# One expert matrix kept in eight pieces in idle rows of the mixer, and its ring slot given to another matrix

## The reference

```
u = rms_norm(x, norm_mix_g[l]) @ w_in[l]
o_a = differential_attention(aq, ak, av, ...)
o_b = hgrn2(bq, bf, bi, bg, lower_bounds[l], hgrn_norm_g[l])
o_c = short_conv(cb, cc, cx, conv_w[l])
x = x + concatenate([o_a, o_b, o_c]) @ w_out[l]
h = rms_norm(x, norm_ffn_g[l])
# each token: one of 4 groups, in it 2 of 8 experts
y_e = (silu(h @ w_gate[e]) * (h @ w_up[e])) @ w_down[e]
x = x + sum of gates * y_e over the token's two experts
```

## Time and profile before

| what | value |
|---|---|
| median of three runs | 1191.2 us |
| the profiled execution's own time | 1192.3 us |
| its span, first to last instruction | 1190.2 us |
| PE busy | 885.7 us, 74% of the span |
| DVE busy | 505.8 us, 42% |
| ACT busy | 171.2 us, 14% |
| POOL busy | 36.9 us, 3% |
| bytes moved | 442.22 MB, mean 372 GB/s |

### The profile page before, as it was taken

How to read it: one execution, slowest core, us unless ns; L and a number is a source line. 1 busy time by engine, 2 the same in 40 slices (tenths; PEclk the granted TensorE clock), 3 DMA queues, 4 the chain that set the end, 5 groups by cost and what they waited for, 6 DMA issues and landing times.

```text
span 1190.2 us, 20391 instructions
## 1 busy us (share of the span) xinstructions
PE 885.7 (74%) x8533; PEld 531.0 (45%) x8533; DVE 505.8 (42%) x1307; ACT 171.2 (14%) x479; POOL 36.9 (3%) x75
## 2 busy tenths in 40 slices
PE   9999997774657574756799999976757575746557
PEld 6577475342324242424465675643424232423234
DVE  2977464332414242424339674643324142424233
ACT  2334211100000000000013441101000000000000
POOL 2011000000000000000000120000000000000000
PEclk9999998888978788978799999988888797888888
DMA  8946389999999999999996273899999999999996
GB/s 276 388 188 249 133 330 426 429 425 428 428 428 428 428 429 428 427 430 425 414 389 260 72 282 124 349 430 427 427 427 428 427 430 428 428 429 428 428 425 282
DMA packets 54700, 442.22 MB, mean 372 GB/s; under 512 B 9312, under 2 KB 12400, under 8 KB 29296
## 3 DMA queue, kind: packets, MB, share of 16 engines
q1 hardware_dynamic: 54640, 441.36, 89.5%
HBM read 440.30 MB, written 1.05 MB: 371 GB/s over the span
## 4 chain that ended last, share of the span: by engine, by line
PE 60%; DMA 27%; DVE 9%; issue 2%; ACT 1%; SPq 1%; DVEq 0%
DMA ring<-in_expert_w_up 26%; PE psum L820 15%; PE psum L835 8%; PE psum L854 8%; PE psum L863 6%; PE psum L938 5%; PE psum L720 5%; PE psum L794 4%; DVE work L1470 2%; PE psum L811 1%; DVE work L1481 1%; PE psum L886 1%; PE psum L955 1%; DVE work L1476 1%; PE psum L738 1%
## 5 line engine op out<-in xcount | busy, mean ns | idle before, releaser
L820 PE MATMUL psum<-ring,work 128*32 128x256 f32 x3712 | 247.8, 426 | 102.9 <-DMA ring<-in_expert_w_up 101.3
L835 PE MATMUL psum<-ring,work 128*32 128x256 f32 x1664 | 144.6, 505 | 131.2 <-DVE work L1476 125.7
L820 PEld LDWEIGHTS psum<-ring,work 128*32 128x32 f32 x3712 | 138.9, 124 | 212.0 <-issue 156.7
L835 PEld LDWEIGHTS psum<-ring,work 128*32 128x32 f32 x1664 | 62.1, 137 | 202.2 <-DVE work L1476 147.8
L1468 DVE TENSOR_SCALAR work<-work 128x128 f32<-128x128 f32 x62 | 14.1, 227 | 312.8 <-ACT work L1142 312.8
L1481 DVE COPY work<-psum 32x256 f32<-32x256 f32 x124 | 52.6, 424 | 158.4 <-PE psum L835 157.3
L854 PE MATMUL psum<-ring,hT 128*128 128x512 f32 x224 | 98.5, 594 | 1.7 <-ACT work L1165 1.7
L720 PE MATMUL psum<-work,h 128*128 128x128 f32 x512 | 66.0, 291 | 32.5 <-DVE work L1434 26.5
L1146 ACT ACTIVATE work<-psum 32x256 f32<-32x256 f32 x124 | 46.2, 373 | 289.1 <-PE psum L835 288.4
L720 PEld LDWEIGHTS psum<-work,h 128*128 128x128 f32 x512 | 62.9, 204 | 45.8 <-DVE work L1434 36.9
L863 PE MATMUL psum<-hT,ring 128*128 128x256 f32 x320 | 70.7, 380 | 0.0
(11 more groups left out here) (289 smaller groups left out, 774.9 us busy)
## 6 DMA issues: line engine op xcount, KB each, us to landing
ring<-in_expert_w_gate SPq DMA_DIRECT2D x64, 2048.0 KB, 18.3
ring<-in_expert_w_up SPq DMA_DIRECT2D x62, 2048.0 KB, 22.6
ring<-in_expert_w_down SPq DMA_DIRECT2D x52, 2048.0 KB, 23.1
ring<-in_w_in SPq DMA_DIRECT2D x10, 2048.0 KB, 18.1
work<-in_expert_w_down SPq DMA_DIRECT2D x6, 2048.0 KB, 21.1
ring<-in_w_out SPq DMA_DIRECT2D x4, 2048.0 KB, 8.1
ring<-in_w_in SPq DMA_DIRECT2D x8, 512.0 KB, 13.4
maps<-in_expert_w_down SPq DMA_DIRECT2D x2, 2048.0 KB, 8.5
```

What stands on the lines that cost most here:

```text
L820: last = T.matmul(bank[GU_BANK[i % 2]][CAP * j:CAP * j + CAP, 0:2 * P], xg[:, k, CAP * i:CAP * i + CAP], gate_up[:, :, k, P * j:P * j + P] ...
L835: last = T.matmul(bank[5][CAP * q:CAP * q + CAP, 0:2 * P], actT[i % 2][:, CAP * j:CAP * j + CAP], down[j][:, 2 * P * q:2 * P * q + 2 * P], ...
```

## The change

In the mixer of each layer SP starts five more transfers. They bring the up matrix of expert 0 in tiles of 512 columns (one for each k of 8) to `up_rows`: rows 4, 5, 7, 11 and 12 of `u` (part of `work`), the two halves of `masks`, and a new tensor `spare`. The first four wait for `lev_sb`, count 9 (the last copy under the masks), the fifth for `oat_ps`, count 2 (`oa_transposes(1)`).

The slot that held up0 now gets gate3, loaded in the mixer at the place in the list where up0 was loaded. Before, gate3 was loaded into slot 2 after the gate product of expert 1. So slot 2 is free earlier, and experts 4 to 7 are placed and ordered anew: gate4 takes that slot, down4 waits for down step 0 alone, down6 waits for up step 4.

```
-        FIRST = [SET_A, (2, AHEAD, IN_MAPS), (0, 1, IN_WORK), (2, XTRA, IN_MAPS)]
-        SECOND = [SET_A, SET_C, SET_B, SET_A]
+        FIRST = [(3, IN_ROWS, 5), (2, AHEAD, IN_MAPS), (0, 1, IN_WORK), (4, XTRA, IN_MAPS)]
+        SECOND = [(2, 3, 5), SET_C, SET_B, SET_A]
+        SECOND_ODD = [(3, 2, 5)] + SECOND[1:]
...
                 e.wait_ge(proj_ps.sem, proj_ps.after(l, projected("bf")))
-                part(ring_full, place(l, FIRST[0][1]), 0, 1)
+                part(ring_full, place(l, FIRST[3][0]), 3, 0)
...
                 part(ring_full, place(l, FIRST[2][2]), 2, 2)
+                up = a["expert_w_up"][l:l + 1, 0:1].rearrange("l e (p k) n -> p (l e k) n", k=KT)
+                full = ring_full[IN_ROWS].sem
+                e.wait_ge(lev_sb.sem, lev_sb.after(l, 9))
+                e.dma_start(up_rows[2], up[:, 2, :]).then_inc(full, 16)
+                e.dma_start(u[:, 11:13, :], up[:, 3:5, :]).then_inc(full, 16)
+                e.dma_start(masks[:, :, :].rearrange("p (k m) n -> p k (m n)", k=2), up[:, 5:7, :]).then_inc(full, 16)
+                e.dma_start(up_rows[7], up[:, 7, :]).then_inc(full, 16)
+                e.wait_ge(oat_ps.sem, oat_ps.after(l, 2))
+                e.dma_start(u[:, 4:6, :], up[:, 0:2, :]).then_inc(full, 16)
                 e.wait_ge(op_ps.sem, op_ps.after(l, 4))
...
                 e.wait_ge(gate_read.sem, gate_read.after(l, 1))
-                part(ring_full, four[0], 4, 0)
+                part(ring_full, gate_slot, 4, four.index(gate_slot))
                 e.wait_ge(gate_read.sem, gate_read.after(l, 2))
-                part(ring_full, place(l, FIRST[3][0]), 3, 0)
-                e.wait_ge(main.gu_ps.sem, main.gu_ps.after(first, 1))
-                part(ring_full, four[1], 4, 1)
+                part(ring_full, place(l, FIRST[1][0]), 4, 1 - four.index(gate_slot))
+                e.wait_ge(main.ye_ps.sem, main.ye_ps.after(first, 1))
+                part(ring_full, four[2], 4, 2)
                 e.wait_ge(main.ye_ps.sem, main.ye_ps.after(first, 2))
                 half_down(slot(IN_MAPS).rearrange("p (j n) -> p j n", j=4)[:, 2:4, :], IN_MAPS, 3, 1)
-                part(ring_full, four[2], 4, 2)
                 part(ring_full, five[0], 5, 0)
...
-                for n in range(3):
-                    part(ring_full, six[n], 6, n)
+                part(ring_full, six[0], 6, 0)
+                part(ring_full, six[1], 6, 1)
                 e.wait_ge(main.gu_ps.sem, main.gu_ps.after(first + 1, 1))
+                part(ring_full, six[2], 6, 2)
                 part(ring_full, seven[0], 7, 0)
```

Three things follow from using these rows. POOL makes the masks again for layer 1, after the first up step of layer 0 has read them (`level_masks`, 23 instructions, the same ones as at the start):

```
+                if l < DEPTH - 1:
+                    again = Chain(masks_again, l)
+                    e.wait_ge(main.gu_ps.sem, main.gu_ps.after(l * GROUPS, 1))
+                    level_masks(e, again)
+                    again.end()
...
                 e.wait_ge(cleared.sem, cleared.after(l, 2))
+                if l:
+                    e.wait_ge(masks_again.sem, masks_again.after(l - 1, MASKS))
```

The matmuls that fill PE's waits in the routing (`keep_warm`) read `x` and no longer `masks`. In `extra_units`, `later` moves to `rstd_row` and is done in two halves, one behind the other; a temporary of the first group moves to row 8:

```
-                        T.matmul(bank[7][:, :], ident[:, :], masks[:, 0:4, :], start=True, stop=True)
+                        T.matmul(bank[7][:, :], ident[:, :], x[:, 0, 0:512], start=True, stop=True)
...
-                    TT(later, upto[0:1, :].unsqueeze(1).to_broadcast([1, MAXX, NE]),
-                       iota[0:1, 0:MAXX].unsqueeze(2).to_broadcast([1, MAXX, NE]), ALU.is_le).then_inc(c.step(), 1)
...
-                    V.tensor_reduce(xe, later, AX, ALU.add).then_inc(c.step(), 1)
-                    e.wait_ge(c.sem, c.last())
+                    for n in range(0, MAXX, HALFX):
+                        TT(later, upto[0:1, :].unsqueeze(1).to_broadcast([1, HALFX, NE]),
+                           iota[0:1, n:n + HALFX].unsqueeze(2).to_broadcast([1, HALFX, NE]), ALU.is_le).then_inc(c.step(), 1)
+                        e.wait_ge(c.sem, c.last())
+                        V.tensor_reduce(xe[:, n:n + HALFX], later, AX, ALU.add).then_inc(c.step(), 1)
+                        e.wait_ge(c.sem, c.last())
```

More of the change, by code:

```diff
@@ L21 @@
 IDENT_MADE = 13
+MASKS = 23
 ONES_MADE = 3
 WARM_UP = 8
-DVE_M = 215
+DVE_M = 217
 DVE_G = 24
@@ L237, in hybrid_trunk @@
         rstd_row = sb("rstd_row", [P, SEQ])
+        later = rstd_row[0:1, 0:SEQ].rearrange("p (m n) -> p m n", n=NE)
+        HALFX = SEQ // NE
+        up_rows = [u[:, 4, :], u[:, 5, :], u[:, 7, :], u[:, 11, :], u[:, 12, :], masks[:, 0:4, :].rearrange("p m n -> p (m n)"),
+                   masks[:, 4:8, :].rearrange("p m n -> p (m n)"), spare[:, :]]
         diag = hg[:, Q_, 0:TI * P].rearrange("p (i t) -> p i t", i=TI)
@@ L305, in hybrid_trunk @@
         ring_full = [sig(f"ring_full{s}", 16 * loads(s, NE - 1))
-                     for s in range(R + 5)]
+                     for s in range(R + 6)]
+        masks_again = sig("masks_again", MASKS)
         up_half = [sig(f"up_half{n}", 16) for n in range(2)]
@@ L631, in gates_and_convolution, with second_blocks, level_masks @@
                 c.end()
+            def second_blocks(n, B):
+                return masks[:, n, :].rearrange("p (b o t) -> p b o t", o=2, t=B)[:, :, 1, :]
+            def level_masks(e, c):
+                nc.gpsimd.memset(masks[:, :, :], 0.0).then_inc(c.step(), 1)
+                e.wait_ge(c.sem, c.last())
+                nc.gpsimd.affine_select(out=masks[:, 0, :], in_=masks[:, 0, :], compare_op=ALU.not_equal, fill=1.0,
+                                        base=0, pattern=[[-1, P]], channel_multiplier=1).then_inc(c.step(), 1)
+                for n, B in enumerate(LEVELS[1:], 1):
+                    nc.gpsimd.memset(second_blocks(n, B), 1.0).then_inc(c.step(), 1)
+                e.wait_ge(c.sem, c.last())
+                for n, B in enumerate(LEVELS[1:], 1):
+                    v = second_blocks(n, B)
+                    nc.gpsimd.affine_select(out=v, in_=v, compare_op=ALU.is_ge, fill=0.0, base=0,
+                                            pattern=[[-2 * B, P // (2 * B)], [0, B]], channel_multiplier=1).then_inc(c.step(), 1)
+                e.wait_ge(c.sem, c.last())
+                for n, B in enumerate(LEVELS[1:], 1):
+                    v = second_blocks(n, B)
+                    nc.gpsimd.affine_select(out=v, in_=v, compare_op=ALU.is_ge, fill=0.0, base=B - 1,
+                                            pattern=[[2 * B, P // (2 * B)], [0, B]], channel_multiplier=-1).then_inc(c.step(), 1)
             made = Chain(const_ok, 0)
@@ L660, in _ @@
                                     base=CHUNK - 1, pattern=[[0, CHUNK]], channel_multiplier=-1).then_inc(made.step(), 1)
[L661 to L677, removed]
-                nc.gpsimd.affine_select(out=v, in_=v, compare_op=ALU.is_ge, fill=0.0, base=B - 1,
-                                        pattern=[[2 * B, P // (2 * B)], [0, B]], channel_multiplier=-1).then_inc(made.step(), 1)
+            level_masks(e, made)
             made.end()
@@ L1092, in _ @@
                 keep_warm(2)
-                first, second, later, final = ([placed(l, slots) for slots in group] for group in (FIRST, SECOND, LATER, LAST))
+                first, second, later, final = ([placed(l, slots) for slots in group] for group in (FIRST, SECOND_ODD if l % 2 else SECOND, LATER, LAST))
                 def unit_loaded(g):
```

30 lines of the change are left out of this document (18 added, 12 removed).

## The result

The changed kernel takes 1183.5 us, the median of four runs (1181.48 to 1184.66); the kernel before takes 1191.1 us in the same comparison. The ratio is 0.9935, with a 95% interval of 0.9918 to 0.9952. So the change gains 7.6 to 8 us. 1181.7 us was forecast, a gain of 9.5 us; the sign, the mechanism and the range hold, and some 1.5 to 1.9 us of the gain are missing.

What follows compares the result with a forecast made beforehand. It took the experts to be bound by bytes and the mixer by PE. Terms of -4.9 us in each layer and +0.3 us for late PE in layer 0 summed to -9.5 us: 1181.7 us, range 1180.4 to 1185.3.

Steps and rivals of the forecast that it cites:

- A matrix out of the full stretch, -4.9 us a layer: Experts' DMA-bound stretch: one matrix fewer to load in each layer saves 4.9 us a layer, provided the queue never runs dry.
- Tiles by about 143 us: Layer 0's mixer: all five tiles of up0 landed by about 143 us, before gate2's start at 148.60.
- Share near 0.6: Last stretch of layer 0's mixer, 130 to 148 us: DMA share near 0.6 after the change, 0.31 before.
- The queue stays full: Experts: despite a matrix less in front, starts keep the queue filled; down4, behind down step 0, can start at about 175.4 us.
- The margins: Experts' starts: time to landing less 7.4 us, each shrinking by 4.9; gate10 left with 0.2 us in layer 0, 2.0 in layer 1.
- PE's wait for up11: Layer 0's experts: PE's wait for this transfer some 18.5 us by the chain, 23.49 before; landing at 286.6 us.
- DVE, +0.5 us for `extra_units`: Just in front of expert 0's activation, both layers: the split comparison and sums cost 0.5 us more, bounds 0.3 and 0.9.
- DVE beside POOL, +0.3 us: Expert 0's activation, layer 0 alone: POOL's mask selects hold DVE for 0.3 us, bounds 0 and 3.3.
- PE late by 0.5 us, 0.3 of it lost: Down0 of layer 0: DVE 0.8 us late, 0.3 hidden, so PE 0.5 late, of which 0.3 exceeds gate10's margin.
- The queue running dry in layer 0: Rival: masks at their upper bound make PE 3.5 us late in layer 0, 3.3 lost: 1184.7 us, chance 0.14.
- Places set the pace: Rival for the experts: starts come just when a place is free, so fewer bytes only idle the DMA: 1191.2 us, chance 0.04.
- The slower clock: Rival: PE at 1.2 GHz in the gather and experts 0 to 3, +8.0 us, 1199.2 us, chance 0.04.

Runs made afterwards that it cites:

- e3_cut: Kernel before with seven eighths of gate3's load left out in both layers, same order of starts: 1188.1 us, 0.9976.
- e6_down4_late: Kernel after with down4 started in its old place, behind down step 1 and the second half of down3: 1189.7 us, 0.9986.
- e12_down4_alone: Kernel before with only down4's start moved behind down step 0, ahead of the half of down3, and all of gate3 loaded: 1192.5 us, 1.0006.
- e1_again: The changed kernel, same program, run again for the spread of its runs: 1183.2 us, 0.9941 to the kernel before.
- e4_warm: Kernel after with six small matmuls of 256 columns in PE's pauses at the layer boundary: 1183.8 us, 0.9939.
- e9_delay_5: Kernel after with six unread matmuls of 512 columns on PE between groups 0 and 1 of both layers: 1185.7 us, 0.9950.
- e2_side: Kernel before with the side edits only (keep_warm reads x, comparison in halves, masks made again beside expert 0): 1191.3 us, 1.0001.
- e8_delay_after: Kernel after with 12 unread matmuls of 512 columns on PE between groups 0 and 1 of both layers: 1194.3 us, 1.0021.
- e11_masks_late: Kernel after with POOL making the masks again one group later, behind the first up step of group 1: 1183.0 us, 0.9924.
- e7_delay_before: Kernel before with 12 unread matmuls of 512 columns on PE between groups 0 and 1 of both layers: 1192.0 us, 1.0009.
- e10_rows_late: Kernel after with the five starts of up0's tiles moved behind gate2, up2 and the half of down3: 1198.1 us, 1.0056.
- e5_cut_early: Kernel before with seven eighths of gate3's load left out and down4 started behind down step 0: 1185.4 us, 0.9944.

## Why the prediction was right, and where the rest is

**What bounds the kernel** was read rightly: a matrix fewer in a stretch with a DMA share of 1.00 made it a matrix shorter.

**A matrix out of the full stretch, -4.9 us a layer**: measured -4.8 and -4.6 in the first profile, -4.6 and -5.3 in the second. Tiles by about 143 us: 144.0. Share near 0.6: 0.63.

**The queue stays full**: yes, but only by down4's start. It was forecast for some 175.4 us plus the kernel's own lateness (gate2 started 0.97 us later than before); it came at 175.94. `e3_cut`, `e6_down4_late` and `e12_down4_alone` together show that neither the bytes nor the start is the gain, but the pair.

**The margins**: forecast for gate10 were 7.4 to 8 us to landing in layer 0 and 9 to 10 in layer 1; measured 10.9 and 10.2. Layer 1 is nearly right. In layer 0 PE was early, not late: in the chain the 1.30 us pause inside down0 is gone, and the scatter of group 0 took 3.69 us in place of 5.29. Neither is work that the change touches, so that layer 0 got through with a margin counted at 0.2 us was luck. For down6 I forecast 9.6 us in layer 0 and measured 12.9 there, 9.2 in layer 1. PE's wait for up11 was to be 18.5 us and is 21.7, since PE came to it early; the landing itself is right, 286.6 forecast, 287.6 with gate2 0.97 us later.

**DVE, +0.5 us for `extra_units`**: 167.54 to 170.03 us is 2.49, where 166.56 to 168.58 was 2.02: +0.47. (The prediction's own sum, 2.1 less 1.67, gives 0.43.)

```profile
167.54 0.29 DVE L1926 TENSOR_TENSOR work<-work 128x128 f32<-128x128 f32 x1
...
168.26 0.40 DVE L1932 TENSOR_TENSOR rstd_row<-work,iota 1x256 f32<-1x256 f32 x1
...
170.03 0.17 DVE L1938 TENSOR_SCALAR work<-work 128x4 f32<-128x4 f32 x1
...
170.23 0.27 DVE L1941 TENSOR_SCALAR xinfo<-work 1x16 int32<-1x16 f32 x1
...
170.82 0.37 DVE L1499 TENSOR_SCALAR work<-work 128x128 f32<-128x128 f32 x1
171.22 0.95 DVE L1501 RECIPROCAL work<-work 128x128 f32<-128x128 f32 x1
```

**DVE beside POOL, +0.3 us**: line 1941 took 0.27 us (0.15 before), line 1499 0.37 and then 0.29 (0.22 and 0.23), together +0.33. POOL at that time:

```profile
170.19 0.29 POOL L661 TENSOR_SCALAR_AFFINE_SELECT masks<-masks 128x128 f32<-128x128 f32 x1
170.43 0.68 POOL L664 MEMSET masks<- 128x64 f32 x7
```

Line 1941 ended at 170.50 us, when the select (170.48) was done. But this is one of two cases. In `e1_again` the same step was held through the select and the seven memsets behind it, to 170.51 us, and took 0.75 us more:

```profile
169.61 0.90 DVE L1941 TENSOR_SCALAR xinfo<-work 1x16 int32<-1x16 f32 x1
...
169.81 0.68 POOL L664 MEMSET masks<- 128x64 f32 x7
```

It took 0.90 us in `e4_warm` and 0.89 in `e9_delay_5` too, and 0.27 or 0.28 in `e2_side`, `e6_down4_late` and `e8_delay_after`. A stretch of over 0.5 us was one of the prediction's signs of being wrong; the term is 0.3 us in some executions and 0.8 in others. The rule of the Trainium skill that the prediction weighed ("SBUF — State Buffer", section "SBUF: two separate sides") agrees with which steps were held: the reciprocal, the products out of PSUM and the transpose kept their times, 0.95, 0.29 and 0.40 us, and it was TENSOR_SCALAR steps that were held. The page lets a step with two SBUF inputs compete only against a GpSimd operation that reads SBUF; here such a step of 256 numbers (line 1932, 0.41 us for 0.40) ran beside a memset, and beside selects only the two small ones of `e1_again` (line 1944, 0.20 us for 0.14, and line 1946, 0.15 for 0.16). These rows hardly test that half. By the rule PE was to be late by at most 1.5 us; the most seen is 0.99.

**PE late by 0.5 us, 0.3 of it lost**: from gate2's start down0 came 0.45 us later in the first profile, 0.99 in `e1_again`, and 0.19 in `e11_masks_late`, where POOL's work is elsewhere. In the first profile nothing of it was lost, since the pause inside down0 went; that was luck too.

**The rivals.** The queue running dry in layer 0 didn't happen there: 1.00 from 168 to 180 us. "Places set the pace" falls with `e7_delay_before`: PE can be 8.3 us late in each layer at a cost of 0.7. The slower clock did not come with the change, but `e10_rows_late` is this rival made real, with its mechanism: a PE that waits 4.8 us in the experts' first step comes back at the lower level, and the thin margin passes it on.

**The mis-sized term** is none of those summed. In the four profiles with the change and all its margins (the first, `e1_again`, `e4_warm`, `e11_masks_late`) the two full stretches are 834.2 to 834.7 us long together; in those of the kernel before and of `e2_side` they are 844.2 and 843.6. That is 8.9 to 10.0 us less, and 9.5 were forecast. What is missing of the gain lies outside the full stretches, where the prediction took nothing to change ("both 4.9 us early ... to the layer's end and through the next mixer"). There the six kernels that load up0 in its old place take 344.7 to 346.5 us, and the seven with its tiles in the mixer's idle time 346.2 to 348.3, by the medians 1.2 us more.

**The margins are the other soft spot**, and they vary from one execution to the next. In the kernel after, layer 1, group 0's scatter was at the lower clock (5.92 us; 3.67 in `e1_again`), down6 started at 794.83, 9.2 us ahead of its landing, and the rate dipped. The first row is of the kernel after, where 354 GB/s cost 0.9 us:

```profile
795.00:800.00 5.00, 2.50 (x24) 1.22 (x28) 2.16 (x5) 0.11 (x1) 0.00 (x0) 0.76 0.96 354
```

In `e1_again`, where down6 had 12.9 us to landing (started at 789.6 us), the rate was 429 GB/s from 790 to 795 us, and this stretch stayed full:

```profile
795.00:800.00 5.00, 4.14 (x74) 2.00 (x64) 1.28 (x4) 1.02 (x3) 0.00 (x0) 0.96 1.00 426
```

So "time to landing less 7.4 us" flatters a margin: starts with 9.2 to 11.2 us to landing lost 0.8 to 1.3 us in some cases (here, in `e5_cut_early`, `e9_delay_5`) and nothing in others (gate10 at 10.2 and 10.9 us in this very profile). That would also fit the wider spread of the single runs, 1181.5 to 1187.0 us, where the kernel before had 1190.3 to 1193.7; that is argued, not shown.

**What stays open** is why it takes 1.2 us more outside the full stretches. The two groups of profiles overlap by 0.3 us, and the time lies elsewhere in each execution. In the first profile 1.0 us of it is no work of the tiles: down2, which SP starts ahead of them, was already 0.99 us late (131.15 for 130.16). At the boundary, line 985 at the lower clock took 1.7 us more. In `e1_again` 0.8 us lies behind the last full stretch. `e2_side`, 344.7 us outside, excludes the side edits; no run separates the rest from the variation between executions.

## What to carry to other kernels

When transfers bound a stretch, move bytes into the idle DMA time of a stretch bound by something else, and move the next start up by as much: the one alone gave 3 us, the other alone nothing, both 6 with seven eighths of a matrix and 8 with a whole one. Each matrix that leaves the stretch takes its length out of the margin of every start behind it, so list for each start the time to landing less that of an empty queue, see which of them get thin, and count a few microseconds as already spent. A piece that an early step waits for is cheap only while it lands ahead of that step: waits of 4.8 and 5.7 us in the two layers cost 15. An added delay is less than its own length where it fills a wait: 10.5 us of matmuls made PE 8.3 us late. And one profile of each kernel is not enough to place a microsecond: outside the full stretches, executions differ by 2.

## What the runs showed of the hardware

- A float32 matmul of 512 columns left two records of 0.43 us; 12 of them took 10.46 us. I had counted one each.
- PE ran at a granted clock of 1.00 from 140 to 164 us in `e10_rows_late` and then stood still for 4.82 us. The next products ran at 0.50, the 1.2 GHz level, and took 3.64 us for what takes 1.96; the mean granted clock from 168 to 180 us was 0.72. In layer 1, behind 5.72 us of idle time, it was the same 3.64 us.
- A pause of 1.30 us inside a run of matmuls, with no wait that the profile shows, was in the trace of before and gone in that of after, whose products at that place are the same. It was 1.10 us in `e7_delay_before`, 0.22 in `e5_cut_early`, and absent in `e3_cut` and `e12_down4_alone`, whose products there are those of before too.
- One float32 TENSOR_SCALAR step of 16 numbers on DVE, which takes 0.15 us alone, took 0.27 or 0.90 us beside POOL's selects and memsets, ending with one or with eight of them.
